# Twenty-two modulation slabs taken out of a feed-forward loop and put between attention and state-space heads

## The chip, the cores and the metric

One core of a Trainium2 chip runs the whole program. The metric is the device time of one execution in microseconds (us); the median of three executions is given. The engines are TensorE (PE, its weight loads are PEld), VectorE (DVE), ScalarE (ACT), GpSimd (POOL) and SyncE (SP), which here does nothing but issue the loads of weights.

## The reference

256 tokens of width 1024 go through two models one after the other, all in fp32. The first has two layers: a mixer (differential attention in layer 0, dilated attention with 16 heads in layer 1), cross-attention to a memory, and a feed-forward block with a gate, a convolution over three tokens and GELU. The second has two layers as well: a bidirectional state-space mixer with 32 heads in 8 groups, then a convolution module, each followed by a SwiGLU block. Each layer of the second model is steered by a *modulation*, which depends on two vectors alone (one for the context, one for the latent tokens) and not on the tokens:

```python
def ada_params(sc, w, b):
    mod = sc @ w + b            # sc (2, 1024), w (1024, 6144)
    return [t[:, None, :] for t in jnp.split(mod, 6, axis=-1)]
# sc = silu(c); one w, b for each of the two layers of the second model
h = h + g1 * mixer(rmsnorm(h, norm_mix_g) * (1 + s1) + sh1)
h = h + g2 * swiglu(rmsnorm(h, norm_ffn_g) * (1 + s2) + sh2)
```

The `w` of one layer is 24 MB. It can be multiplied at any time before that layer begins. Layer 1 of the second model begins after the state-space layer and its SwiGLU.

## The kernel before

**Slabs.** All weights lie in DRAM as 1 MB slabs of 128 partitions x 2048 floats, in the order of use. `STAGES` lists the stages and `SOURCE` the slab of each place of the stream. SP brings the stream through a ring of four buffers (`ring`). A slab is requested when PE has begun the third slab before it (`slab_begun`, counted by `begun`), so three are ahead. One slab of `ada_w` holds 256 of its 6144 columns: 24 slabs for each layer.

**Exact products.** Big projections are made of three fast passes. ACT copies a slab rounded into `w_hi` (`hi`, L2827, in two halves), POOL subtracts it from the slab into `w_lo` (`lo`, L2219, in two halves), and PE adds hi x hi, hi x lo and lo x hi (L1708, L1710, L1712): 48 matmuls of 256 columns a slab (`col_T_split`, or `col_N_split` for the other orientation; `rows_split`, L1763, for output rows). `w_lo` lies on top of the ring. In `col_T_split` the first output half takes all eight depth tiles, then the second output half does; PE waits for the first half of `w_lo` before depth tile 0 and for the second before tile 4 of the first output half. `col_N_split` waits for both halves at once.

**The modulation** isn't split. `ada` multiplies a slab as plain fp32 with a stationary operand of 32 columns (two of them hold `sc`), eight matmuls in four 32-row strips of a bank (L1939). One slab gives 2 x 256 numbers in four partial sums; DVE transposes them (`turn_ada`, L2465), ACT copies the used columns to `modC` (`ada_out`, L2880), and at the end `ada_columns` adds the strips on PE, and `modulation` adds the bias on DVE.

**Where it stands.** `f0` and `f1` are the first model's feed-forward stages, 22 slabs of its own each. Their stream alternates: one modulation slab, one feed-forward slab, 22 times; the last two of the 24 are loaded to one side (`aside`) and multiplied while a norm is computed (`late_ada`, L1950). So layer 0's modulation is in `f0`, layer 1's in `f1`. As a modulation slab has no low part, the low part of the feed-forward slab is written over its place in `w_hi` and the ring buffer is released by `lo_ready`. DVE and ACT do for each feed-forward slab: three convolution taps (L2445, L2447, L2449), GELU (L2906), product (L2454), `h_hi` (L2909), `h_lo` (L2457). `fo1` (L1763) follows. The same loop without modulation is `h0`, the SwiGLU after the state-space layer.

**Dilated heads** (loop over `q` in 0..10): for pair `q` PE makes scores (L2116) in banks 0 to 3, DVE adds the bias and takes the maximum (L2711), ACT exponentiates (L3026), DVE scales (L2727), PE transposes the weights (`weights_to_keys`, L2098, banks 4 and 5) for pair `q - 2`, ACT copies them out (L2751), and PE multiplies them with the values (L2136) for pair `q - 3` in bank 6 or 7. The output projection `rows("gwo")` (L1813) waits until banks 6 and 7 are free.

**State-space heads** (loop over head `q` in 0..31, group `g = q // 4`, place `j = q % 4`): PE makes sums (`sums`, L1442), a quarter of the gate projection (`gate_part`, L1455, plain fp32; 16 matmuls a group, into bank 3 or 7 by turns), at `j` 1 turns tokens (L1466), at `j` 2 makes scores (L1474), and at odd `j` the outputs of two heads (`two_heads`, L1493). DVE: `bounded` (L812), `head` (L824, L827), at `j` 2 `combine` (L836, L846) and `inputs_of` (L786), at `j` 3 `masked_scores` (L798). ACT: `decays` (L1134 and L1140, Exp), at `j` 3 `turned` (L1104, L1107), and at `j` 0 after `decays` the gate's Silu of the group before (`gate_of`, L1124). Silu and Exp need different tables.

## Time and profile before

| | |
|---|---|
| median of 3 executions | 2055.17 us (2053.49 to 2056.4) |
| profiled execution | 2055.43 us, its span 2053.7 us |
| busy in the span | PE 1920.8 us (94%), POOL 1252.0 (61%), DVE 1109.8 (54%), ACT 998.6 (49%) |
| moved by DMA | 342.30 MB, mean 167 GB/s |
| granted clock of TensorE | 0.977 of full speed over the span |

The profile is of one execution. PE's busy time is modelled, since matmuls overlap, so a matmul of "280 ns" may follow the one before it by less than half of that; the pitch between starts is what counts. fp32 matmuls leave two records each. Idle time of an engine counts only where the engine is the one that is waited for, which the chain of work that ended last shows.

### The profile page before, as it was taken

How to read it: one execution, taken by the hardware profiler on the slowest of the kernel's cores; microseconds unless marked ns; L12 is line 12 of the kernel's file. 1: busy time of each engine (PE TensorE's matmuls, PEld its weight loads, DVE VectorE, ACT ScalarE, POOL GpSimd, SP SyncE). 2: the span in 40 equal slices, each digit the busy share in tenths (PEclk: the TensorE clock that was granted, in tenths of full speed). 3: DMA queues.
4: the chain of work that ended last, by engine and by line, in shares of the span. 5: the costliest groups of instructions: out<-in, count | busy, mean ns of one | idle time of the engine just before them, and what ended most of it. 6: DMA issues, size and time to landing. Idle time of an engine off the chain costs nothing.

```text
span 2053.7 us, 34088 instructions
## 1 busy us (share of the span) xinstructions
PE 1920.8 (94%) x13629; PEld 1700.4 (83%) x13629; DVE 1109.8 (54%) x1524; ACT 998.6 (49%) x1726; POOL 1252.0 (61%) x585
## 2 busy tenths in 40 slices
PE   7989999999999989989999899898789999999997
PEld 7879799887999866868888788876579988968996
DVE  5472346623700172146667655678728962847981
ACT  4654345543444373435543444377845545525542
POOL 8768467686888405456778344300369886417995
PEclk9999999999999999999999899999999999999999
DMA  7435377774555405357764122211245554324552
GB/s 259 144 129 203 120 269 308 303 264 167 185 186 185 143 1 183 146 218 299 313 257 146 64 81 86 99 64 62 82 154 184 184 185 147 120 82 159 195 187 104
DMA packets 49217, 342.30 MB, mean 167 GB/s; under 512 B 5264, under 2 KB 7312, under 8 KB 8144
## 3 DMA queue, kind: packets, MB, share of 16 engines
q1 hardware_dynamic: 47440, 331.02, 44.1%
q0 software_dynamic: 1664, 9.70, 1.2%
q8 instruction: 80, 1.31, 0.3%
q14 instruction: 33, 0.27, 0.0%
HBM read 339.65 MB, written 1.05 MB: 166 GB/s over the span
## 4 chain that ended last, share of the span: by engine, by line
PE 77%; DVE 11%; ACT 6%; POOL 3%; issue 2%; DMA 1%; DVEq 0%; SPq 0%; ACTq 0%; POOLq 0%
PE bank L1708 13%; PE bank L1712 13%; PE bank L1763 13%; PE bank L1710 12%; PE bank L1813 3%; PE bank L1743 2%; PE bank L1742 2%; PE bank L1740 2%; PE bank L1939 2%; PE bank L1309 2%; PE bank L1311 2%; PE bank L1312 2%; ACT arena L1140 2%; DVE arena L723 2%; PE bank L1531 1%
## 5 line engine op out<-in xcount | busy, mean ns | idle before, releaser
L2219 POOL TENSOR_TENSOR w_lo<-ring,w_hi 128x1024 fp32r<-128x1024 f32 x360 | 877.0, 2465 | 275.2 <-ACT w_hi L2827 258.0
L1708 PE MATMUL bank<-x_hi,w_hi 128*128 128x256 f32 x2176 | 618.5, 284 | 18.6 <-POOL w_lo L2219 14.1
L1712 PE MATMUL bank<-x_lo,w_hi 128*128 128x256 f32 x2176 | 619.7, 285 | 0.0
L2827 ACT ACTIVATE w_hi<-ring 128x1024 fp32r<-128x1024 f32 x448 | 448.9, 1052 | 332.8 <-DMA ring<-slabs_dram 326.1
L1708 PEld LDWEIGHTS bank<-x_hi,w_hi 128*128 128x128 f32 x2176 | 415.8, 191 | 38.5 <-issue 37.3
L1712 PEld LDWEIGHTS bank<-x_lo,w_hi 128*128 128x128 f32 x2176 | 415.0, 191 | 0.0
L1710 PE MATMUL bank<-x_hi,w_lo 128*128 128x256 f32 x1472 | 414.3, 281 | 0.0
L1710 PEld LDWEIGHTS bank<-x_hi,w_lo 128*128 128x128 f32 x1472 | 282.4, 192 | 0.0
L2219 POOL TENSOR_TENSOR w_hi<-ring,w_hi 128x1024 fp32r<-128x1024 f32 x88 | 208.8, 2394 | 102.7 <-ACT w_hi L2827 102.7
L2751 ACT ACTIVATE arena<-bank 128x512 f32<-128x512 f32 (+1 forms) x178 | 97.9, 563 | 279.6 <-PE bank L1712 192.1
L1710 PE MATMUL bank<-x_hi,w_hi 128*128 128x256 f32 x704 | 197.5, 281 | 0.0
L416 POOL TENSOR_TENSOR w_lo<-ring,w_half 128x1024 fp32r<-128x1024 f32 x32 | 77.7, 2432 | 112.8 <-ACT w_half L1027 112.7
L1710 PEld LDWEIGHTS bank<-x_hi,w_hi 128*128 128x128 f32 x704 | 133.3, 189 | 0.0
L723 DVE SCALAR_TENSOR_TENSOR arena<-bank,pt,arena 128x508 f32<-128x508 f32 (+3 forms) x128 | 87.2, 682 | 60.1 <-ACT arena L1042 56.5
L1763 PE MATMUL bank<-w_hi,h_hi 128*128 128x512 f32 x352 | 111.9, 395 | 4.1 <-POOL w_lo L2219 1.9
L1763 PE MATMUL bank<-w_lo,h_hi 128*128 128x512 f32 x352 | 111.4, 394 | 0.0
L1763 PE MATMUL bank<-w_hi,h_lo 128*128 128x512 f32 x352 | 111.1, 393 | 0.0
L2432 DVE TENSOR_TENSOR arena<-arena 128x256 f32<-128x256 f32 x44 | 96.9, 2202 | 23.8 <-ACT arena L2899 14.5
L2457 DVE TENSOR_TENSOR h_lo<-arena,h_hi 128x256 f32 (+1 forms) x44 | 90.6, 2059 | 33.3 <-ACT h_hi L2909 33.3
L1309 PE MATMUL bank<-s_hi,w_half 128*128 128x512 f32 (+1 forms) x288 | 104.7, 363 | 1.9 <-DVE s_lo L655 1.9
L2711 DVE CUSTOM_DVE_ANT_0 arena<-bank,dist 128x512 f32<-128x512 f32 x32 | 22.1, 692 | 148.9 <-PE bank L2116 148.3
L1312 PE MATMUL bank<-s_hi,w_lo 128*128 128x512 f32 (+1 forms) x288 | 102.2, 355 | 0.0
(355 smaller groups left out, 3665.1 us busy)
## 6 DMA issues: line engine op xcount, KB each, us to landing
ring<-slabs_dram SPq DMA_DIRECT2D x308, 1024.0 KB, 4.8
lnrow<-ln_dram POOLq DMA_DIRECT2D x6, 1024.0 KB, 5.3
arena<-slabs_dram SPq DMA_DIRECT2D x4, 1024.0 KB, 8.3
xt<-xT_dram SPq DMA_DIRECT2D x1, 1024.0 KB, 5.9
xt<-memT_dram SPq DMA_DIRECT2D x1, 1024.0 KB, 12.0
x<-x_dram SPq DMA_DIRECT2D x1, 1024.0 KB, 13.6
arena<-ctx_dram POOLq DMA_DIRECT2D x1, 1024.0 KB, 8.0
lnrow<-ln_dram POOLq DMA_DIRECT2D x2, 512.0 KB, 5.0
```

Source lines behind the costliest of these rows:

```text
L723: ins = v.scalar_tensor_tensor(out=d3[:, :, lo:hi], in0=s3[:, :, lo + o:hi + o], scalar=pt[:, scw + k * 32 + j:scw + k * 32 + j + 1], in1= ...
L1309: ins = pe.matmul(dst, wh[:, k, :], hi_(k), start=(k == 0), stop=False)
L1312: ins = pe.matmul(dst, wl[:, k, :], hi_(k), start=False, stop=(k == KC - 1))
L1708: ins = pe.matmul(dst, wh[:, k, c], src[0][:, k, :], start=(k == 0), stop=False)
L1710: ins = pe.matmul(dst, wl[:, k, c], src[0][:, k, :], start=False, stop=False)
L1712: ins = pe.matmul(dst, wh[:, k, c], src[1][:, k, :], start=False, stop=(k == KC - 1))
L1763: ins = pe.matmul(bank[2 * tt + h][:, :], st, w[:, k, h * 512:(h + 1) * 512], start=(first and n == 0), stop=(end and n == 2))
L2219: pool.tensor_tensor(dst[:, c], ring[:, s, c], w_hi[:, s, c].bitcast(F32), ALU.subtract).then_inc(S["lo_ready"], 1)
L2432: step(v.tensor_tensor(act[:, u, :], act[:, u, :], val, ALU.mult))
L2457: v.tensor_tensor(h_lo[:, j, :], act[:, u, :], h_hi[:, j, :].bitcast(F32), ALU.subtract).then_inc(S["hT_ready"], 1)
L2751: a.activation(dst, bank[b][:, :] if src is None else src, ACT.Copy if not kw else ACT.Identity, **kw).then_inc(free["act"][b], 1)
L2827: a.activation(w_hi[:, g % RING, c], ring[:, g % RING, c], ACT.Copy) \
```

## The change

Layer 0's modulation stays where it is. Layer 1's 24 slabs leave `f1`:

- ten (`a1`) are multiplied in the dilated heads, one at the head of each of the iterations 0 to 9;
- two stay aside and are multiplied during the norm as before (`late_rows`);
- twelve (`sa0` to `sa7`, two and one by turns) are multiplied in the state-space heads at `j` 0. The gate projection has `j` 1 to 3 instead of 0 to 3 (5, 5 and 6 of its 16 matmuls) and bank 3 alone, and ACT's `gate_of` stands ahead of `decays` at `j` 0.

`sc_in` is laid out with zeros on both sides, so that a window of 32 columns puts the two `sc` columns at any of 16 places (`sc_at`); the sums of up to 16 slabs gather in one bank. Each group of slabs then needs one copy by ACT, two small matmuls by PE (`columns_of`) and one bias addition by DVE (`mod_rows`), in place of a transpose and a copy for each slab. In the dilated heads bank 7 holds the sums, so that L2136 has bank 6 alone.

`f1` becomes a plain stage like `h0`: 22 slabs, low parts in `w_lo`. POOL's low parts around it: slab 0's is made before the two calls of `rstd` of that norm, slab 1's after them; before, the first feed-forward slab's stood ahead of them, at the second place of the stream.

Apart from that, `col_T_split` and `col_N_split` go by depth halves: the first four depth tiles of both output halves, then the last four of both.

```diff
+def ada_slab(layer, j):
+    return AT[f"f{layer}"] + (2 * j if j < FC else 2 * FC + j - FC)
+DIL_ADA = 10
+LATE_ADA = (10, 11)
+HEAD_ADA = [2, 1, 2, 1, 2, 1, 2, 1]
...
+    if _name == "gwo":
+        STAGES.append(("a1", [ada_slab(1, j) for j in range(DIL_ADA)]))
+    if _name == "sz":
+        for _g, _k in enumerate(HEAD_ADA):
+            STAGES.append((f"sa{_g}", [ada_slab(1, _next + u) for u in range(_k)]))
+            STAGES.append((f"sz{_g}", [AT["sz"] + _g]))
+            _next += _k
+    elif _name == "f1":
+        STAGES.append((_name, [AT["f1"] + 2 * u + 1 for u in range(FC)]))
...
+        def sc_at(k, place):
+            return sc_in[:, 32 * k + 30 - 2 * place:32 * k + 62 - 2 * place]
...
+        def mod_group(v, L, b, first, n):
+            v.wait_ge(full["dve"][b], L.filled(b))
+            mod_rows(v, b, 0, first, n).then_inc(free["dve"][b], 1)
+            v.wait_ge(free["dve"][b], L.freed(b))
...
             for q in range(SH + 4):                     # ACT, state-space heads
                 g, j = q // 4, q % 4
+                if j == 0 and g >= 1:
+                    gate_of(g - 1)
                 if q < SH:
                     decays(q)
                 if j == 3 and g + 1 < SG:
                     across_scores(g + 1)
-                if j == 0 and g >= 1:
-                    gate_of(g - 1)
+                if q == SH - 2:
+                    copy_out(7, head_kept, bank[7][:, 0:T])
...
-                zb, ch = (3, 7)[g % 2], j // 2          # PE, gate_part
-                for k in range(4 * (j % 2), 4 * (j % 2) + 4):
+                for n in range((0, 5, 10)[part], (5, 10, 16)[part]):
...
                 sums(q)
-                gate_part(g, j)
+                if j == 0:
+                    modulation_part(g)
+                else:
+                    gate_part(g, j - 1)
...
             for j in range(6):                          # PE, swo
+                if j == 2:
+                    pe.wait_ge(free_of(7), frees(7))
+                    fill(columns_of(head_kept, 7, 0), 7, "dve")
...
-                for ch in range(2):                     # col_T_split
-                    col_T_half(stage, u, ch, b, src, used_up, waits, last_net)
+                for at in (0, HC):
+                    for ch in range(2):
+                        col_T_half(stage, u, ch, b, src, used_up, waits, last_net,
+                                   range(at, at + HC), True)
...
+            def ada_into(b, w, place, first, end):
+                for k in range(KC):
+                    q = 32 * (k % 4)
+                    ins = pe.matmul(bank[b][q:q + 32, 0:256], sc_at(k, place), w[:, k, :],
+                                    start=(first and k < 4), stop=(end and k >= 4))
+                    begun(ins, k == 0)
+                return ins
+            def columns_of(kept, b, at):
+                for c in range(2):
+                    ins = pe.matmul(bank[b][:, at + 32 * c:at + 32 * (c + 1)],
+                                    kept[:, c * P:(c + 1) * P], pick, start=True, stop=True)
+                return ins
...
-                    for u in range(4):                  # PE, network
-                        ada(stage, 2 * u, u, 2 * i)
-                        col_T_split(stage, 2 * u + 1, u, waits=turned if u == 0 else None)
+                if layer:
+                    with L.rounds(5, per):
+                        for u in range(4):
+                            col_T_split(stage, u, u, waits=turned if u == 0 else None)
...
             for q in range(pairs + 3):                  # PE, dilated heads
+                if q < DIL_ADA:
+                    ins = ada_into(7, slab("a1", q).rearrange("p (k c) -> p k c", k=KC), q, q == 0,
+                                   q == DIL_ADA - 1)
+                    if q == DIL_ADA - 1:
+                        fill(ins, 7, "act")
...
-                    b = 6 + k % 2
+                    k, b = q - 3, 6
...
-            rows("gwo", 4, goT)
+            rows("gwo", 4, goT, hook=dil_columns)
...
                 if k == 4:                              # POOL
-                    lo("f1", 1)
+                    lo("f1", 0)
                 rstd()
                 rstd()
+                if k == 4:
+                    lo("f1", 1)
...
-                    if conv is not None:                # DVE, network
+                    if conv == 0:
                         turn_ada(u)
...
-                    ada_out(u, j)                       # ACT, network
+                    if layer == 0:
+                        ada_out(u, j)
...
+            copy_out(7, dil_kept, bank[7][:, 0:T])      # ACT, after the dilated heads
```

## Rows read from the trace of the kernel before

**Rows 1.** The page, section 4: shares of the chain that ended last, by engine.
```profile
PE 77%; DVE 11%; ACT 6%; POOL 3%; issue 2%; DMA 1%; DVEq 0%; SPq 0%; ACTq 0%; POOLq 0%
```

**Rows 2.** Windows: stretch, length; busy us PE, PEld, DVE, ACT, POOL; clock, DMA, GB/s.
```profile
700.00:771.00 71.00, 57.07 (x558) 48.07 (x557) 46.82 (x130) 45.69 (x107) 0.00 (x0) 0.93 0.05 16
901.00:1047.00 146.00, 145.48 (x1344) 129.98 (x1344) 89.46 (x124) 73.14 (x114) 98.26 (x42) 0.99 0.78 305
1340.00:1482.00 142.00, 121.53 (x784) 91.78 (x782) 113.08 (x163) 113.58 (x283) 18.09 (x11) 1.00 0.19 68
```

**Rows 3.** The chain that ended last, in f1: start, us, what.
```profile
930.75 1.00 PE bank L1939 x16
937.60 1.00 PE bank L1939 x16
```

**Rows 4.** Timeline of one slab of f1 (start, us, engine).
```profile
946.22 0.54 DVE L2445 TENSOR_SCALAR arena<-bank,pt 128x256 f32<-128x256 f32 x1 [0.19 <-DVE arena L2465]
947.40 4.75 POOL L2219 TENSOR_TENSOR w_hi<-ring,w_hi 128x1024 fp32r<-128x1024 f32 x2 [2.14 <-ACT w_hi L2827]
949.89 2.53 DVE L2457 TENSOR_TENSOR h_lo<-arena,h_hi 128x256 f32 x1 [0.79 <-ACT h_hi L2909]
```

**Rows 5.** Timeline of h0: the same step of two slabs in a row.
```profile
1583.61 0.43 DVE L2432 TENSOR_TENSOR arena<-arena 128x256 f32<-128x256 f32 x1 [0.21 <-DVE h_lo L2434]
1589.17 0.42 DVE L2432 TENSOR_TENSOR arena<-arena 128x256 f32<-128x256 f32 x1
```

**Rows 6.** Timeline of the norm ahead of f1.
```profile
884.56 4.75 POOL L2219 TENSOR_TENSOR w_hi<-ring,w_hi 128x1024 fp32r<-128x1024 f32 x2 [6.21 <-ACT w_hi L2827]
890.09 0.75 DVE L2385 SCALAR_TENSOR_TENSOR x<-bank,small,lnrow 128x512 f32<-128x512 f32 x1 [2.22 <-POOL small L2198]
```

**Rows 7.** Timeline of PE at the start of fo1.
```profile
1057.73 0.70 PE L1763 MATMUL bank<-w_hi,h_hi 128*128 128x512 f32 x2 [0.35 <-DVE arena L2454]
```

**Rows 8.** Timeline of PE in the dilated heads.
```profile
715.62 2.03 PE L2116 MATMUL bank<-arena 64*128 64x256 f32 x24 [1.86 <-DVE small L2711]
724.62 3.58 PE L2116 MATMUL bank<-arena 64*128 64x256 f32 x24
738.66 2.03 PE L2116 MATMUL bank<-arena 64*128 64x256 f32 x24
744.91 2.03 PE L2116 MATMUL bank<-arena 64*128 64x256 f32 x24
759.20 1.06 PE L2098 MATMUL bank<-ident,arena 128*128 128x128 f32 x8 [1.74 <-ACT arena L2751]
```

**Rows 9.** Timeline of the state-space heads, one group: ACT, then PE, DVE.
```profile
1384.40 0.60 ACT L1134 ACTIVATE dist<-bank 128x512 f32<-128x512 f32 x1 [2.87 <-DVE arena L812]
1388.69 0.60 ACT L1134 ACTIVATE dist<-bank 128x512 f32<-128x512 f32 x1 [0.44 <-DVE arena L812]
1390.97 1.28 ACT L1124 ACT_TABLE_LOAD   x1
1392.88 1.28 ACT L1134 ACT_TABLE_LOAD   x1
1387.06 1.89 PE L1455 MATMUL bank<-xlat,ring 128*128 128x256 f32 x8
1388.79 0.60 PE L1466 MATMUL bank<-ident,arena 128*128 128x128 f32 x4
1390.47 1.08 PE L1493 MATMUL bank<-xt,arena 128*64 128x256 f32 x8 [1.08 <-DVE tri L827]
1392.78 0.51 PE L1442 MATMUL bank<-acT,pair_sum 128*128 128x256 f32 x2
1393.93 0.69 DVE L812 TENSOR_TENSOR arena<-bank,arena 128x512 f32<-128x512 f32 x1
```

**Rows 10.** The chain of the same group: the step that follows.
```profile
1396.55 0.97 DVE arena L827
```

**Rows 11.** Timeline of PE at the very start of the program.
```profile
23.48 0.39 PE L1708 MATMUL bank<-x_hi,w_hi 128*128 128x256 f32 x1 [0.94 <-POOL w_lo L2219]
```

More of the change, by code:

```diff
@@ L1118, in gate_of @@
             def gate_of(g):
-                zb = (3, 7)[g % 2]
-                a.wait_ge(full["act"][zb], L.filled(zb))
+                a.wait_ge(full["act"][3], L.filled(3))
                 if g >= 2:
                     a.wait_ge(S["ssq_ready"], g - 1)
-                a.activation(ring_z[g % 2], bank[zb][:, :].rearrange("p (c t) -> p c t", c=2),
-                             ACT.Silu).then_inc(free["act"][zb], 1)
-                L.freed(zb)
+                a.activation(ring_z[g % 2], bank[3][:, :].rearrange("p (c t) -> p c t", c=2),
+                             ACT.Silu).then_inc(free["act"][3], 1)
+                L.freed(3)
             def decays(q):
@@ L1938, in ada, with late_rows @@
                     q = 32 * (k % 4)
-                    ins = pe.matmul(bank[b][q:q + 32, 0:256], sc_in[:, k, :], w[:, k, :],
+                    ins = pe.matmul(bank[b][q:q + 32, 0:256], sc_at(k, 0), w[:, k, :],
                                     start=(k < 4), stop=(k >= 4))
                 fill(ins, b, "dve")
+            def ada_into(b, w, place, first, end):
[10 more added lines that the diff above has]
+                return ins
+            def late_rows(e):
+                pe.wait_ge(aside_landed[e], 32)
+                if e == 0:
+                    pe.wait_ge(free_of(7), frees(7))
+                for k in range(KC):
+                    q = 32 * (k % 4)
+                    ins = pe.matmul(bank[7][q:q + 32, 0:256], sc_at(k, e), aside[e][:, k, :],
+                                    start=(e == 0 and k < 4), stop=(e == 1 and k >= 4))
+                if e == 1:
+                    fill(ins, 7, "act")
+                    marks["late_rows"] = L.now(("act", 7))
             def late_ada(layer, e):
@@ L1971, in ada_columns @@
                                         start=True, stop=True)
+                    else:
+                        ins = pe.matmul(part[:, 0:2 * FC, :], pick, kept[:, q, 0:2 * FC, :],
+                                        start=True, stop=True)
+                if layer:
+                    pe.wait_ge(free["act"][7], marks["late_rows"])
+                    ins = columns_of(late1_kept, 4, 128)
                 fill(ins, 4, "dve")
@@ L2268, in _ @@
                 if k == 4:
-                    marks["lo_f1"] = L.now(("took", "hi_ready"))
-                    lo("f1", 1)
+                    lo("f1", 0)
                 rstd()
@@ L2790, in x_to_T @@
                             late_out(tt)
+                        if rows_at and b == 7:
+                            copy_out(7, late1_kept, bank[7][:, 0:T])
                         a.wait_ge(full["act"][b], L.filled(b))
@@ L2913, in network @@
                     L.n.update({("product", b): done[b] for b in range(4)})
-                    L.n.update({("turned", b): done[b] for b in (5, 6)})
                     per = {(k, b): 1 for k in ("net", "product") for b in range(4)} | {
-                        ("turned", 5): 2, ("turned", 6): 2, ("took", "pre_ready"): 4}
-                    hi(net, 3)
+                        ("took", "pre_ready"): 4}
+                    if layer == 0:
+                        L.n.update({("turned", b): done[b] for b in (5, 6)})
+                        per |= {("turned", 5): 2, ("turned", 6): 2}
+                        hi(net, 3)
                 else:
```

215 lines of the change are left out of this document (125 added, 90 removed).

## The prediction

> **What bounds the kernel now.** I read the page first, then a table of windows by stage, then inside the stages that the change touches the chain of waits and the timeline. The chain that ended last is 77% PE [rows 1], and the windows tell the stages apart [rows 2]. In `f1` PE is busy for 145.48 of 146 us while the next engine, POOL, has 98.26: there PE's work is the time, and what is taken out shortens it until another engine comes up. In the dilated heads (57.07 of 71 us) and the state-space heads (121.53 of 142) PE has gaps, so one might think that slabs go in for nothing. But a busy share says nothing on where the gaps lie; that takes the timelines.
>
> **f1: what goes.** In the chain a modulation slab's matmuls begin at 930.75 and 937.60: one pair of slabs takes 6.85 us, 1.00 of it the modulation's [rows 3]. What is the pitch without it? `h0` is the same loop with the same 48 matmuls a slab; its product on DVE comes at 1583.61 and 1589.17, pitch 5.56 [rows 5]. That is 1.29 less, more than the 1.00: the change between the two kinds of matmul costs too. I take 5.56: 22 x (6.85 - 5.56) = **28.4 us less**.
>
> Will another engine hold `f1` above 5.56? POOL needs 4.75 a slab [rows 4]. The stream needs one load of 1 MB in 5.56 us where it now has two in 6.85 at 305 GB/s [rows 2]. DVE is the one to look at: from the first tap of a slab at 946.22 to the end of `h_lo` at 949.89 + 2.53 = 952.42 it takes 6.20 us in one string [rows 4], with waits for ACT inside, and DVE takes the slabs strictly in turn. Laid end to end, these strings would hold `f1` at 6.20. But look at `h_lo` itself: 2.53 us for 256 columns, where the first tap of as many columns takes 0.54. It starts 2.49 us after POOL's pair of subtractions and ends 0.27 after them (947.40 + 4.75 = 952.15): it stands waiting for POOL's second subtraction to end [rows 4]. So its end hangs on POOL's beat, not on its own start; it can start up to about 2 us later for nothing. With POOL at one pair a slab, DVE lags by 0.8 us and stays there. (The Trainium skill, "SBUF — State Buffer", Who interferes with whom, says the same in general: a VectorE instruction with two SBUF inputs and a GpSimd one that reads SBUF exclude each other, and the second to be issued waits for the whole of the first. By that rule alone one could also fear that each `h_lo` costs DVE a full subtraction, which makes the first rival below; the row's end, just behind POOL's, agrees with the rule and not with that fear.)
>
> **Around f1.** In the norm ahead, POOL does its two subtractions from 884.56 to 889.31 and only then the `rstd` that DVE waits 2.22 us for [rows 6]. The new order asks for slab 0's low part before it, and as the stream has no modulation slab ahead, that slab is requested one slab of output rows earlier and POOL is done with it in time: **-2.2**. At the end of `f1` PE now waits 0.35 us for DVE's last product [rows 7]; with DVE 0.8 behind and PE's last slab not followed by anything to cover that, I take **+0.9**. The late slabs, the columns and the addition of the bias stay beside the norm and the output rows. Sum for `f1`: -29.7.
>
> **Dilated heads: what comes.** Scores start at 738.66 and 744.91, 6.25 us a pair [rows 8]. The cycle is: scores, DVE's maximum, ACT's exponential and copy, PE's transposes, scores again. Each waits for the one before, and the slab is put between transposes and scores, on that cycle: 1.00 an iteration at the price of [rows 3]; the ends are 0 (a gap covers it) and 1.29. It is covered where PE waits anyway right there or just before: 1.86 us at `q` 2, about as much at `q` 1, and 1.74 ahead of the transposes of `q` 8 [rows 8]. Seven of ten remain: +7.0. Then `rows` waits for bank 7 too, whose copy is ACT's last: half the width of the 0.60 us read in [rows 9], so +0.4; two matmuls of 32 columns, +0.2 (four of 128 take 0.60, [rows 9]). Against this stands the clock: it is 0.93 over this stage [rows 2], and scores that take 2.03 us took 3.58 in one of the stretches at half clock [rows 8]. All of it is worth (1 - 0.93) x 71 x 0.8, 4 us. Slabs in the gaps before `q` 1 and 2 may remove some: -1.0. Together **+6.6**; DMA moves 16 GB/s here [rows 2], so that a slab every 7 us is there in time.
>
> **State-space heads.** The slab itself comes after PE's sums at `j` 0, in the place of 1.9 us of gate work; what counts is the single bank 3. PE may begin the gate's next part only after ACT's Silu of the group before. ACT, counted from the start of `decays` at `j` 3 (1384.40): it has finished `turned` at 1388.69 - 0.44, after 3.85 us; the gate's table and Silu take 1392.88 - 1390.97 = 1.91; bank 3 is free at 5.76. Until then PE has the end of two heads (by which it runs some 1.8 behind that start once a group has this order), twice the sums (0.51 each) and one or two slabs (1.00 each): 4.8 at most. **The slabs cost nothing** here. From 5.76 PE does five matmuls (ten records at (1388.79 - 1387.06) / 8: 2.16), the tokens (0.5), two heads (1392.78 - 1390.47 = 2.31) and the sums of `j` 2 (0.51), with starts in between 0.1: 11.34. DVE bounds them and multiplies, 0.69 and 0.03 twice: its L827 starts at 12.78 [rows 9]. Before, it started at 1396.55, after 12.15 [rows 10]. So a group grows by 0.63, seven times: +4.4; behind L827 all is as before. ACT's own path gets shorter by the 0.44 that it waited. With one copy on ACT and two small matmuls again (+0.6): **+5.0**. Ends: 7 x -0.44 = -3.1, if PE keeps up, and 12.0 for the slabs on top.
>
> **Depth halves.** At the start PE waits 0.94 us for POOL's fourth half, with 12 of 48 matmuls of that slab done [rows 11]; with 24 to do before that wait, it is gone: **-0.9**. Elsewhere PE doesn't wait for a second half, and the order costs nothing: the matmuls are the same.
>
> **Sum.** Loop -28.4, norm -2.2, end +0.9, so -29.7; with +6.6, +5.0 and -0.9 that is -19.0 on the profiled execution's 2055.43 (its span is 2053.7, the rest lies around it), thus 2036.4; the median of the runs, 2055.17, is 0.3 below that execution. I say **2036.3 us**.
>
> **Rivals.**
> 1. *DVE's string sets f1* (6.20 a slab, above): the loop saves 14.3 instead of 28.4: 2050.4. For it: 6.20 is measured; against: the end of `h_lo` hangs on POOL. Chance 0.14.
> 2. *The gaps take everything:* PE keeps up in the state-space heads (-3.1 instead of +4.4) and the dilated heads get the whole clock back (3 more): 2025.8. For it, PE's gaps in [rows 2]; against, the walk above. 0.09.
> 3. *The slabs cost their full price in the state-space heads too,* because their PE time delays sums that DVE needs: +12, 2048.3. PE has 121.53 of 142 us filled already. 0.11.
> 4. *Slower:* the gate on ACT now stands ahead of `decays`. Should bank 3 be filled only after ACT arrives, ACT stands at the head of its queue, and DVE and PE, which need the decays, behind it. Then gate, table (1.28), slabs (1.5 a group) and 0.63 add up: 5.3 x 7 = 37 instead of 4.4: 2069. It decides against the change from 3.9 us a group on ((19.0 + 4.1) / 7 + 0.63). Against it: the last gate part ends more than 4 us before ACT gets there. 0.04.
>
> Rivals 1 and 3 together (2062) have 0.02; my forecast 0.60, by itself 2030 to 2042.
>
> **Range and chances.** From rival 2 to rival 1: 2026 to 2051. Under 0.2% (4.1 us) is no change that a measurement of this kernel can tell. Faster: forecast, rivals 2 and 3 and most of 1, 0.89; within: the rest of 1 and mixtures of 1 with parts of 3, 0.05; slower: 0.06.
>
> **What would show it.** In the profile after: starts of a `f1` slab 5.56 us apart (6.2 would be rival 1) with `h_lo` ending just behind POOL's pair; scores of the dilated heads 7.2 us apart; PE waiting for ACT before the first gate part of a group and L827 0.6 later per group, no wait of ACT for bank 3; `rstd` ahead of `f1` without DVE's 2.2 us; no wait for POOL in the second slab of the program. I would be wrong by most if DVE and POOL fall into another beat in `f1`.

## The result: slower, and the profile after

The changed kernel takes 2067.05 us (median; 2066.77 to 2069.39), the kernel before on the same chip 2054.49: ratio 1.0063, 95% interval 1.0045 to 1.0080. That is 12.6 us slower where I had forecast 19 less. The profiled execution has a span of 2064.7 us, against 2053.7.

The stages show where it went. Each number is the start of the first matmul of a stage on PE's timeline, in us. The third column is the run of the first experiment, told below, and the fourth the best kernel of the study.

| stage begins | before | after | arena back | best |
|---|---|---|---|---|
| last values ahead of the dilated heads (`gv`) | 682.25 | 689.47 | 681.55 | 681.82 |
| `xv1`, behind the dilated heads | 798.16 | 810.07 | 803.53 | 803.90 |
| `f1` | 903.39 | 911.02 | 902.57 | 902.95 |
| `fo1` | 1054.37 | 1040.70 | 1026.64 | 1027.06 |
| `h0`, behind the state-space heads | 1534.39 | 1532.03 | 1518.99 | 1507.35 |
| `ho0` | 1660.17 | 1662.30 | 1643.67 | 1632.86 |
| `h1` | 1855.79 | 1860.20 | 1840.86 | 1830.46 |
| `ho1` | 1981.28 | 1991.73 | 1966.62 | 1954.92 |
| span | 2053.7 | 2064.7 | 2039.1 | 2027.4 |

`f1` did become shorter, by 21.3 us (150.98 to 129.68). But time is lost in places where no work was added: 7.2 us ahead of the dilated heads, 4.5 in `h0`, 6.0 in `h1`. To see why, look at one stretch in which PE never waits, eight slabs of `gq` and `gk`: 384 matmuls, then the first of the next projection. PE's timeline of before:

```profile
570.47 0.28 PE L1708 MATMUL bank<-x_hi,w_hi 128*128 128x256 f32 x1
614.84 0.28 PE L1740 MATMUL bank<-w_hi,x_hi 128*128 128x256 f32 x1
```

and of after:

```profile
573.92 0.28 PE L1768 MATMUL bank<-x_hi,w_hi 128*128 128x256 f32 x1
620.40 0.28 PE L1806 MATMUL bank<-w_hi,x_hi 128*128 128x256 f32 x1
```

44.37 / 384 is 115.5 ns from one matmul to the next; 46.48 / 384 is 121.0. Same instructions, same count, the full granted clock in both. Each one's own duration (0.28) does not show it; only the distance between starts does. The changed kernel multiplies 114 slabs of this kind: 114 x 48 x 5.5 ns is 30 us. The 16 slabs of the other orientation (`col_N_split`) went the other way: the four behind this stretch take 23.04 us before (614.84 to 637.88) and 22.61 after (620.40 to 643.01), 120.0 and 117.8 ns a matmul. The wide matmuls changed too, whose code is untouched: the chain of `ho0` of before, of after, and of a later run (the arena 64 bytes lower), one row each.

```profile
1660.17 59.91 PE bank L1763 x258
```

```profile
1662.30 60.44 PE bank L1831 x258
```

```profile
1656.39 58.76 PE bank L1831 x258
```

That untouched code changed its pace was the hint that the order of the matmuls is not it.

The rest of the profile after, against the forecast. The chain that ended last, by engine, with 75% on PE where it had 77% [rows 1]:

```profile
PE 75%; DVE 10%; POOL 5%; issue 4%; ACT 4%; DMA 1%; DVEq 0%; POOLq 0%; SPq 0%; ACTq 0%
```

In `f1`, POOL's pair of subtractions and DVE's `h_lo` of one slab [rows 4]: `h_lo` stretches to 965.24 and ends 0.28 us behind the pair (960.19 + 4.77). DVE still hangs on POOL's beat, as forecast. The loop takes 129.68 / 22 = 5.89 us a slab, where I had 5.56.

```profile
960.19 4.77 POOL L2339 TENSOR_TENSOR w_lo<-ring,w_hi 128x1024 fp32r<-128x1024 f32 x2 [1.03 <-ACT w_hi L2949]
963.21 2.03 DVE L2577 TENSOR_TENSOR h_lo<-arena,h_hi 128x256 f32 x1 [0.80 <-ACT h_hi L3032]
```

In the norm ahead of `f1` [rows 6], POOL is done early and DVE's first product with `rstd` follows without a wait for it:

```profile
891.45 4.76 POOL L2339 TENSOR_TENSOR w_lo<-ring,w_hi 128x1024 fp32r<-128x1024 f32 x2 [0.60 <-ACT w_hi L2949]
900.51 0.75 DVE L2505 SCALAR_TENSOR_TENSOR x<-bank,small,lnrow 128x512 f32<-128x512 f32 x1
```

In the dilated heads [rows 8] scores are 7.25 us apart, where they were 6.25:

```profile
740.05 2.02 PE L2229 MATMUL bank<-arena 64*128 64x256 f32 x24
747.30 2.02 PE L2229 MATMUL bank<-arena 64*128 64x256 f32 x24
754.54 2.03 PE L2229 MATMUL bank<-arena 64*128 64x256 f32 x24
```

In the state-space heads [rows 9, 10] the chain goes from ACT's Silu (L1165, first its table) to PE's gate (L1499). A group with two slabs, then one with a single slab:

```profile
1392.34 1.28 ACT L1165
1393.63 0.61 ACT xt L1165
1394.38 2.40 PE bank L1499 x10
1396.77 0.44 PE bank L1519 x4
1397.21 2.31 PE bank L1546 x24
...
1447.93 1.28 ACT L1165
1449.22 0.61 ACT xt L1165
1449.96 4.03 PE bank L1499 x10
1453.99 2.31 PE bank L1546 x24
```

PE's timeline has its wait for the Silu in the same two groups:

```profile
1394.38 2.40 PE L1499 MATMUL bank<-xlat,ring 128*128 128x256 f32 x10 [1.51 <-ACT xt L1165]
1449.96 4.03 PE L1499 MATMUL bank<-xlat,ring 128*128 128x256 f32 x10 [2.37 <-ACT xt L1165]
```

The same ten records (five matmuls) take 2.40 us and 4.03: there PE comes back at half its clock (1.2 GHz). This happens in two of the six groups that wait, both with one slab and a wait of some 2.4 us; the third such group (at 1376.40) kept the full clock, and so did all three with two slabs and a wait of 1.51. And at the output projection behind these heads, whose first slab began at the full clock in the kernel before, PE stands for 5.08 us and then is slow again. PE's timeline, and the chain from there:

```profile
1469.11 1.19 PE L1587 MATMUL bank<-w_swo,yT_hi 128*128 128x512 f32 x2 [5.08 <-ACT xt L1165]
```

```profile
1469.11 7.95 PE bank L1587 x24
1477.06 2.31 PE bank L1546 x24
1479.37 5.79 PE bank L1587 x24
```

### The profile page after: what moved, and what is told of

It reads as the page before. It is cut to its first block, busy times and chain, and to the rows that moved or that the text cites. A ratio compares the mean times of both kernels' runs of the same rounds, so it can differ in the third digit from the quotient of the medians.

```text
span 2064.7 us, 33951 instructions
## 1 busy us (share of the span) xinstructions
PE 1945.6 (94%) x13633; PEld 1728.1 (84%) x13633; DVE 1007.8 (49%) x1502; ACT 996.1 (48%) x1703; POOL 1249.3 (61%) x585
## 4 chain that ended last, share of the span: by engine, by line
PE 75%; DVE 10%; POOL 5%; issue 4%; ACT 4%; DMA 1%; DVEq 0%; POOLq 0%; SPq 0%; ACTq 0%
PE bank L1831 13%; PE bank L1768 12%; PE bank L1771 11%; PE bank L1774 11%; POOL w_lo L2339 4%; PE bank L1881 3%; PE bank L1809 2%; PE bank L1811 2%; PE bank L1806 2%; PE bank L1353 2%; PE bank L1355 2%; PE bank L1356 2%; PE bank L1587 2%; DVE arena L765 2%; PE bank L1499 1%
## 5 line engine op out<-in xcount | busy, mean ns | idle before, releaser
L2339 POOL TENSOR_TENSOR w_lo<-ring,w_hi 128x1024 fp32r<-128x1024 f32 x404 | 979.4, 2452 | 329.3 <-ACT w_hi L2949 311.7
L1768 PE MATMUL bank<-x_hi,w_hi 128*128 128x256 f32 x2176 | 628.4, 289 | 17.2 <-POOL w_lo L2339 13.0
L1771 PE MATMUL bank<-x_hi,w_lo 128*128 128x256 f32 x1824 | 520.8, 286 | 0.0
L1768 PEld LDWEIGHTS bank<-x_hi,w_hi 128*128 128x128 f32 x2176 | 419.5, 193 | 27.8 <-issue 27.7
L1771 PEld LDWEIGHTS bank<-x_hi,w_lo 128*128 128x128 f32 x1824 | 351.9, 193 | 0.0
L2339 POOL TENSOR_TENSOR w_hi<-ring,w_hi 128x1024 fp32r<-128x1024 f32 x44 | 104.5, 2397 | 48.5 <-ACT w_hi L2949 48.5
L1355 PE MATMUL bank<-s_lo,w_half 128*128 128x512 f32 (+1 forms) x288 | 102.0, 354 | 0.0
L1771 PE MATMUL bank<-x_hi,w_hi 128*128 128x256 f32 x352 | 98.8, 281 | 0.0
L497 POOL TENSOR_TENSOR dist<-dist,xt 128x512 f32<-128x512 f32 x8 | 10.6, 1325 | 144.4 <-ACT xt L1146 144.4
L2577 DVE TENSOR_TENSOR h_lo<-arena,h_hi 128x256 f32 (+1 forms) x44 | 78.2, 1777 | 33.6 <-ACT h_hi L3032 33.6
```

The costliest lines, as they stand in the source:

```text
L1355: pe.matmul(dst, wh[:, k, :], lo_(k), start=False, stop=False)
L1768: ins = pe.matmul(dst, wh[:, k, c], src[0][:, k, :], start=(k == 0 and (ch == 0 or not both)), stop=False, skip_group_check=both)
L1771: ins = pe.matmul(dst, wl[:, k, c], src[0][:, k, :], start=False, stop=False, skip_group_check=both)
L2339: pool.tensor_tensor(dst[:, c], ring[:, s, c], w_hi[:, s, c].bitcast(F32), ALU.subtract).then_inc(S["lo_ready"], 1)
L2577: v.tensor_tensor(h_lo[:, j, :], act[:, u, :], h_hi[:, j, :].bitcast(F32), ALU.subtract).then_inc(S["hT_ready"], 1)
```

## Experiments on the place of the arrays

`w_hi` and `x_hi` (the rounded weights and activations), `h_hi` and `h_lo` lie in the arena; the remainders `w_lo` and `x_lo` lie in the slab ring and in the triangle tile, which are allocated before `small` and did not move. The conditioning tile `sc_in` grew from 256 to 286 floats and `small` shrank from 576 to 552. After rounding up to 32 bytes the arena begins at byte 114,656 instead of 114,624. Four kernels tell this place from the order of the matmuls.

**Arena back** (e1; changed kernel, constants packed):

```diff
-small = sb("small", [P, 552])
+small = sb("small", [P, 544])
-pick = small[:, 264:296]
+pick = small[:, 248:280]
-lamp = small[:, 296:424]
+lamp = small[:, 280:408]
-dtn = small[:, 296:552]
+dtn = small[:, 280:536]
```

> The changed kernel, with the small constants packed 8 floats tighter, so that the turned latent and the arena (w_hi, x_hi, h_hi and most else) lie at the byte they had before the change; the changed kernel has them 32 bytes further (114,656 in place of 114,624 bytes), because the conditioning tile grew from 256 to 286 floats and the small tile shrank by 24 only. No instruction differs. Theory place (the 32 bytes make the split projections' matmuls start every 121.0 instead of 115.6 ns): the triples of L1768 go back to 0.347 us, 114 slabs x 48 x 5.4 ns = 29.5 us less, so about 2038 us. Theory order (multiplying by halves of the depth makes them slow): same as the changed kernel, 2067 us within 2.

Measured: 2040.99 us, ratio 0.9946 (0.9930 to 0.9963). It computes with the same instructions as the changed kernel at other addresses, and it is faster than the kernel before.

**The new order in the kernel before** (e3; its `col_T_half`, `col_T_split`, `col_N_split` replaced by the changed kernel's):

```diff
-for ch in range(2):
-    col_T_half(...)
+for at in (0, HC):
+    for ch in range(2):
+        col_T_half(..., range(at, at + HC), True)
```

> The kernel before with the depth-half order of the split projections alone (both output halves of one bank in turn for depth chunks 0 to 3, then for 4 to 7), nothing else. Theory order: its 92 projection slabs outside the two feed-forwards go from 115.6 to 121.0 ns a matmul, 92 x 48 x 5.4 ns = 24 us more, about 2078 us. Theory place: the pitch stays at 115.6 ns, and the start comes out 0.9 us sooner, 2053.5 us within 1.5.

Measured: 2053.67 us, ratio 0.9998 (0.9989 to 1.0008), the same stretch at 115.6 ns (44.38 / 384). The order slows nothing.

**The kernel before, arena 32 bytes on** (e2):

```diff
-small = sb("small", [P, 576])
+small = sb("small", [P, 584])
```

> The kernel before with the small tile 8 floats longer and no other edit, so that the turned latent and the arena start 32 bytes further, where the changed kernel has them. Theory place: 92 slabs x 48 x 5.4 ns = 24 us more, less 18 slabs x 48 x 2.1 ns = 1.8 us in the projections with tokens as columns, plus some 2 ns in each of about 1,000 wide matmuls, so about 2078 us. Theory order: no difference, 2054.5 us within 2.

Measured: 2075.01 us, ratio 1.0103 (1.0087 to 1.0120), 121.0 ns. Eight unused floats cost this kernel some 21 us.

**The old order in the changed kernel** (e4; the second edit reversed; every address as changed):

> The changed kernel with its split projections in the order of the kernel before (all eight depth chunks of one output half, then of the other), everything else and every address as changed. Theory order: the pitch goes back from 121.0 to 115.6 ns, 114 x 48 x 5.4 ns = 29.5 us less, plus the 0.9 us of the start, about 2039 us. Theory place: 121 ns stays, 2068 us within 2. If both had a part, this run and the one with the arena back would share the 29 us between them.

Measured: 2072.22 us, ratio 1.0091 (1.0074 to 1.0108), 121.0 ns. Theory order falls. The old order is even 5 us worse by the medians, more than the 0.9 of the start, though the two intervals touch (1.0074 to 1.0108 against 1.0045 to 1.0080). The same with the arena back (e5):

> The changed kernel with the arena back at its old byte and the split projections in the order of the kernel before (one output half, then the other). Compared with the changed kernel whose arena is back (2041.0 us), it is the order of the matmuls alone. In the changed kernel with the arena 32 bytes on, the old order cost 5.2 us (2072.2 against 2067.0), in the kernel before the new order gave nothing (2053.67 against 2053.65). Theory wait (the new order lets a projection begin on half a slab where the remainders of the weights are only just done, which is so now that the first-layer loop runs at 5.6 us a slab): about 2045 to 2046 us. Theory none (what the arena's place added is gone, and with it what the order gave): 2041 us within 1.5.

Measured: 2047.30 us, ratio 0.9961 (0.9948 to 0.9973), against 0.9946 (0.9930 to 0.9963): 3 us by the ratios, 6 by the medians, with intervals that overlap, so that its size is not settled. Its `f1` begins 2.2 us later than with the new order and ends 6.5 later (1033.16); in that loop PE waits for GpSimd's subtraction of `w_lo` five times, 2.2 us in all, which the new order's loop does not do. In the kernel before, a slab of modulation stood between two projections; I read it as what gave POOL that time, but no run separates this.

Then: which array, and what about 32 bytes?

**`w_hi` alone** (e8; on the arena-back kernel):

```diff
-arena = sb("arena", [P, 28672])
+arena = sb("arena", [P, 28680])
-w_hi = part("w_hi", arena_at + 4 * 20480, RING, SLAB)
+w_hi = part("w_hi", arena_at + 4 * 20488, RING, SLAB)
```

> The changed kernel with the arena back (2041.0 us), and of its arrays w_hi alone (the rounded weights) 32 bytes further, the arena 8 floats longer for it; x_hi, m_hi, h_hi and all else stay. Theory stationary (the projections with tokens as rows of the result load their weights from w_hi, and this load is what the 32 bytes slow): the pitch of L1768 to L1774 goes from 115.6 to 121 ns, 114 x 48 x 5.4 ns, so about 2067 us. Theory moving (it is the moving operand, x_hi of 1 KB a partition): the pitch stays at 115.6 ns, about 2041 us, and only the wide matmuls of L1831, where w_hi is the moving operand, take 2 ns more, 1 to 2 us in all.

Measured: 2051.38 us, ratio 0.9985 (0.9975 to 0.9994), 117.8 ns. Neither theory: 10 of the 26 us by the medians, 8 of 24 by the ratios.

**All of the arena 64 bytes lower** (e10; constants packed by 16 floats more), and, with `w_hi` put back on the byte it had in the arena-back kernel, **`x_hi` alone** 32 bytes off its own (e9; the rest of the arena stays 64 bytes lower):

```diff
-small = sb("small", [P, 544])
+small = sb("small", [P, 528])
```

```diff
-x_hi = part("x_hi", arena_at + 4 * 18432, KC, T)
+x_hi = part("x_hi", arena_at + 4 * 18440, KC, T)
-w_hi = part("w_hi", arena_at + 4 * 20480, RING, SLAB)
+w_hi = part("w_hi", arena_at + 4 * 20496, RING, SLAB)
```

> The changed kernel with its small constants packed tighter still, so that the turned latent and the arena start 64 bytes below the place that gave 2041.0 us, and 96 below the changed kernel's. Theory boundary (what counts is whether the arrays begin on a multiple of 64 bytes): pitch 115.6 ns and 2041 us within 2. Theory distance (it is the distance to the arrays that did not move, the weights' and the activations' remainders, in the slab ring and the triangle tile): another pitch, 118 to 121 ns, 2050 us or more.

> The changed kernel with the arena on a 64-byte boundary (2041.0 us with it 32 bytes back), and x_hi alone, the rounded activations that are the moving operand of the projections, 32 bytes off that boundary; w_hi lies 64 bytes further than in that kernel, all the rest 64 bytes lower. With w_hi alone 32 bytes off the boundary the pitch went from 115.6 to 117.8 ns and the time to 2051.4. Theory sum (each operand that lies 32 bytes off costs its own part): the pitch goes to 118 to 119 ns, 114 x 48 x 2.4 to 3.4 ns = 13 to 19 us, so 2054 to 2060 us. Theory pair (it is w_hi and x_hi standing 32 bytes off the two remainders, or off each other, that counts): anything from 2041 to 2051 us; equal to the 2051.4 us of w_hi alone if only their distance matters.

Measured: 2057.23 us, ratio 1.0012 (1.0002 to 1.0021), and 2055.86 (2053.44 to 2064.32), 1.0011 (0.9999 to 1.0022), both at 120.0 ns. In e9 the pitch is above what either theory gave, though the time lies in the range of theory sum. `x_hi` alone, 32 bytes lower, costs 4.5 ns, where `w_hi` alone, 32 higher, cost 2.3 and both 32 higher 5.5; no run has `x_hi` alone 32 higher, so it stays open whether such parts add up. The first, e10, ends the notion of a 64-byte boundary: moved by 64 bytes, the projections are slow again, while the wide matmuls become faster than in any kernel so far (58.76 us for 258, the third row above). Its stretch on PE's timeline:

```profile
573.54 0.28 PE L1768 MATMUL bank<-x_hi,w_hi 128*128 128x256 f32 x1
619.62 0.28 PE L1806 MATMUL bank<-w_hi,x_hi 128*128 128x256 f32 x1
```

Is it the place of an array, or its distance from the ones that stayed? Two kernels on the fastest version (told in the next section) move the others; 64 bytes taken out of the constants leave the arena at byte 114,624:

```diff
+sb("pad", [P, 16])
 ring_at = aligned()        # e13: ring, triangle tile and all between
```

```diff
+sb("pad", [P, 16])
 tri_at = aligned()         # e14: triangle tile (x_lo) and what follows it
```

> The kernel of 2029.7 us (arena back, gate late, last heads first) with 64 bytes put ahead of the slab ring and 64 taken out of the small constants, so that ring (w_lo), triangle tile (x_lo) and all between lie 64 bytes further and the arena (w_hi, x_hi, h_hi, h_lo) where it was, at byte 114,624. The distance between the rounded arrays and the remainders is now as in the kernel whose arena lay 64 bytes lower (2057.2 us, every triple's matmuls 120.0 ns apart), while w_hi and x_hi lie at the byte that gave 115.6 ns. Theory distance: 120.0 ns a matmul in the projections and 227 ns in the wide ones, 16 us more than 2029.7, about 2046 us. Theory place (the byte of w_hi and x_hi themselves): 115.6 ns and 2030 us within 2.

> As the run before it, but the 64 bytes stand ahead of the triangle tile, behind the slab ring: x_lo lies 64 bytes further, w_lo, w_hi and x_hi lie where the kernel of 2029.7 us has them. Theory distance of the moving pair (x_hi against x_lo): the pitch is 120.0 ns or near it, about 2046 us. Theory distance of the weights' pair (w_hi against w_lo), or place: 115.6 ns stays, 2030 us within 2. Part of each would give a time between. The wide matmuls of the feed-forwards read neither of the two and stay at 231 ns in every case.

Measured: 2047.63 us, ratio 0.9958 (0.9941 to 0.9975), 120.0 ns; and 2041.68, 0.9929 (0.9912 to 0.9945), 117.8 ns, against 0.9880 for the base. So it is largely the distance: with `w_hi` and `x_hi` at the byte that was good, but `w_lo` and `x_lo` 64 bytes further, 18 us by the medians are lost (16 by the ratios), and the pace is that of e10, whose arrays have the same distances at other bytes. The other orientation and the wide matmuls agree with e10 as well (table). The wide ones of e13 in the chain:

```profile
1648.94 58.76 PE bank L1831 x258
```

It is not the weights' pair alone that decides, since moving `x_lo` alone costs 12 of the 18 us (10 of 16), though it touches only one of the pairs; theory distance of that pair alone, with 120.0 ns, is not borne out either. What e13 shows in PE's timeline:

```profile
575.29 0.28 PE L1768 MATMUL bank<-x_hi,w_hi 128*128 128x256 f32 x1
621.37 0.28 PE L1806 MATMUL bank<-w_hi,x_hi 128*128 128x256 f32 x1
```

All in one table; "pitch" is the length of the stretch from its first matmul to the first of the next projection, divided by 384, from the same two rows in each run's timeline. "Other" is the same for the 192 matmuls of the other orientation behind it, and "wide" the time of the 258 wide matmuls of `ho0` in the chain. The offsets are the start bytes modulo 128, a unit that I chose because 114,624 and 16,512 differ by 64 in it; the runs do not prove that it is the period.

| run | w_hi | x_hi | w_lo | x_lo | pitch, ns | other, ns | wide, us |
|---|---|---|---|---|---|---|---|
| before, arena back, e3, best | 64 | 64 | 0 | 0 | 115.5 to 115.6 | 120.0 | 59.87 to 59.91 |
| e8 | 96 | 64 | 0 | 0 | 117.8 | 117.2 | 59.60 |
| e14 | 64 | 64 | 0 | 64 | 117.8 | 117.8 | 59.89 |
| e9 | 64 | 32 | 0 | 0 | 120.0 | 117.8 | 60.02 |
| e10 | 0 | 0 | 0 | 0 | 120.0 | 120.0 | 58.76 |
| e13 | 64 | 64 | 64 | 64 | 120.0 | 120.0 | 58.76 |
| after, e2, e4 | 96 | 96 | 0 | 0 | 121.0 | 117.8 | 60.43 to 60.44 |

## Experiments on the state-space heads

With the arena back, the stretch from `fo1` to `h0` still takes 492.35 us where it took 480.02: +12.3, for which I had +5.0.

**One bank for the gate, alone, in the kernel before** (e6). No slabs:

```diff
-zb, ch = (3, 7)[g % 2], j // 2         # four matmuls in each of the four steps
+for n in range((0, 5, 10)[part], (5, 10, 16)[part]):   # bank 3, steps 1 to 3
 ...
-                if q < SH:
-                    decays(q)
                 if j == 0 and g >= 1:
                     gate_of(g - 1)
+                if q < SH:
+                    decays(q)
```

> The kernel before with one part of the change alone: in the state-space heads the gate's projection has bank 3 for every group and no longer banks 3 and 7 in turn, sixteen matmuls in steps 1 to 3 of a group (5, 5, 6) and none in step 0, and ScalarE's Silu stands ahead of the decays of a group's first head and not behind them. No slab is multiplied there, all else as before. Theory bank (the single bank, on which TensorE waits until the Silu of the group before has read it, is what costs the changed kernel 12 us in these heads): the group's period goes from 17.06 to about 17.9 us, 7 x 0.9 = 6 us, with up to two groups longer by 1.6 at half clock, so 2060 to 2063 us. Theory slabs (the slabs' 1.0 us in a group's step 0 is what costs): 2054 to 2055 us. My forecast had 4.4 us for the gate's part, 2058 us.

Measured: 2074.08 us, ratio 1.0096 (1.0079 to 1.0113): 19.7 us slower than before, more than with the slabs (+12.3 in this stretch), and more than theory bank gave. The chain and PE's timeline of one group:

```profile
1411.49 0.61 ACT xt L1122
1412.23 4.60 PE bank L1453 x10
1416.84 0.85 PE bank L1464 x4
1417.69 2.32 PE bank L1491 x24
...
1432.83 4.61 PE bank L1453 x10
```

```profile
1412.23 4.60 PE L1453 MATMUL bank<-xlat,ring 128*128 128x256 f32 x10 [3.08 <-ACT xt L1122]
```

PE waits 3.08 us for the Silu (1.51 with two slabs, 2.37 with one), and from here on every group's ten records behind it run at half clock; the groups are 20.60 us long. Of the three groups before, the one that waited only 0.93 us ran at full clock. The windows of the heads give the granted clock (the column behind the engines' busy times), of this kernel, of after, and of the next one:

```profile
1344.00:1493.00 149.00, 123.44 (x718) 94.11 (x718) 108.30 (x156) 107.33 (x274) 13.96 (x9) 0.88 0.15 53
```

```profile
1343.00:1470.00 127.00, 110.27 (x795) 82.68 (x794) 97.82 (x141) 96.32 (x244) 14.18 (x10) 0.96 0.36 136
```

```profile
1330.00:1449.00 119.00, 108.51 (x802) 81.04 (x800) 100.89 (x143) 95.50 (x246) 14.49 (x9) 1.00 0.41 150
```

The modulation slabs, put where PE would else have waited, kept the clock up in four of six groups. The slabs are not what costs: they hide part of what the new gate costs. This edit has three parts, though (one bank, no gate work in step 0, the Silu ahead of the decays); the next two runs leave the bank and the Silu where they are and move the gate's matmuls.

**The gate in a group's last two steps** (e7, arena back):

```diff
-for n in range((0, 5, 10)[part], (5, 10, 16)[part]):
+for n in range(8 * part, 8 * part + 8):
 ...
-if j == 0:
-    modulation_part(g)
-else:
-    gate_part(g, j - 1)
+if j < 2:
+    modulation_part(g, j)              # one slab a step
+else:
+    gate_part(g, j - 2)
```

> The changed kernel with the arena back (2041.0 us), and in the state-space heads a group's slabs in steps 0 and 1 (one in each) and its gate in steps 2 and 3, eight matmuls each, in place of slabs in 0 and gate in 1, 2, 3. TensorE then reaches bank 3 some 4 us after the Silu has read it and does not wait there. Theory bank (the wait for the Silu at the gate's first matmul is on the path): the heads give back 0.9 us in each of 7 groups and the two stretches at half clock, 6 to 9 us in all, 2032 to 2035 us. Theory work (TensorE's work of a group is the bound whatever its order, or the Silu is late by the gate's last part instead): 2039 to 2043 us.

Measured: 2035.25 us, ratio 0.9908 (0.9891 to 0.9924). Most groups are 16.81 us long (17.06 before), at a clock of 1.00. The single bank and the Silu's place are as they were; a second slab now stands in step 1. The same on the kernel before, without slabs (e12):

> The kernel before with the gate of the state-space heads in one bank (no slabs there), its sixteen matmuls in a group's last two steps, eight each; with them in steps 1 to 3 this kernel took 2074.1 us and TensorE's granted clock was 0.88 there. Theory wait (what costs is that TensorE stands waiting for the Silu and comes back at half clock; where the gate comes late enough, a single bank costs nothing but at the end): groups of about 17 us at a clock of 1.00, and some 5 us at the output projection, which still waits for bank 3: 2058 to 2061 us. Theory work (without the slabs, steps 0 and 1 leave TensorE so little to do that the clock falls anyway): groups of 18 to 20 us and 2065 us or more.

Measured: 2064.46 us (2061.59 to 2065.85), ratio 1.0049 (1.0033 to 1.0066). 10 us better than e6, from which it differs in the place of the gate's matmuls alone: half of what e6 cost was the wait at the bank and the slow clock behind it, and neither the one bank by itself nor the Silu's place. But it is 3.5 to 6.5 above what theory wait gave. Its groups are as long as theory wait had them (17.82 and 16.38 us by turns, 17.1 in the mean), and PE waits 5.0 us at the output projection; but the clock is 0.96 over its heads, where theory wait had 1.00: in every second group two heads' matmuls (24 records) take 4.07 us instead of 2.31. Theory work had the fall of the clock right, and the length of the groups not. In the profiled executions the same order takes 486.04 us from `fo1` to `h0` with slabs (e7) and 488.61 without.

**The last heads first** (e11). In the kernel with the late gate PE still stands at the output projection:

```profile
1449.03 1.19 PE L1587 MATMUL bank<-w_swo,yT_hi 128*128 128x512 f32 x2 [5.05 <-ACT xt L1165]
```

```diff
+two_heads(SH // 2 - 1)
 for b_ in (0, 1, 2, 3):
     pe.wait_ge(free_of(b_), frees(b_))
 ...
-if j == 1:
-    two_heads(SH // 2 - 1)
```

> The kernel with the arena back and the gate in a group's last two steps (2035.3 us), and one edit: the last two heads' matmuls stand ahead of the output projection of the state-space layer, where they stood behind its first slab. There TensorE sat idle for 5.05 us, because this projection begins by waiting for banks 0 to 3, and bank 3 is free only when ScalarE's last Silu has read it (in the kernel before, the last gate was in bank 7); then it ran its first 24 matmuls in 8.54 us in place of 5.74, at a granted clock of 0.73, and the last heads, on which the last four weight roundings wait, came 8 us after the Silu. Theory bank (this wait is the part of the one-bank gate that the other order left): the last heads run in the idle time, GpSimd's roundings have no gap of 5.3 us, and 4 to 5.5 us are given back, so 2030 to 2031 us. Theory end (the projection ends with four roundings that wait for slabs from memory, whatever came before): 2034 to 2036 us.

Measured: 2029.70 us, ratio 0.9880 (0.9863 to 0.9896): 25 us faster than the kernel before, 37 faster than the changed one. PE's timeline at the same place, with the last heads in the gap:

```profile
1446.40 1.08 PE L1546 MATMUL bank<-xt,arena 128*64 128x256 f32 x8 [2.66 <-DVE tri L869]
...
1448.80 0.70 PE L1588 MATMUL bank<-w_swo,yT_hi 128*128 128x512 f32 x2
```

From `fo1` to `h0` it is now 480.29 us: with twelve modulation slabs in them, this stretch takes as long as it did without. The kernel before does not have this place of the last heads, and no run gives it one; what it would save there is open.

## Why the prediction was wrong

- **The step that failed** is one sentence: "Elsewhere PE doesn't wait for a second half, and the order costs nothing: the matmuls are the same." That the order costs nothing holds (e3). But "the matmuls are the same" priced 5472 matmuls at nothing because their instructions don't change, and the sum has no term for the diff's two allocation lines. They moved the operands by 32 bytes, and this costs 26 us by the medians (2067.05 against 2040.99), 24 by the ratios. The sum by the rows is 30. In the three loops `f1`, `h0` and `h1` it comes out: 17.0 us of 17.4. The other 48 slabs should give 12.7, and the rest of the program differs by 8.6; 1.7 of the gap are the 16 slabs of the other orientation, which became faster, and what remains was not traced. The pitch of 5.56 that I carried from `h0` into `f1` fell with it: 48 matmuls at 121.0 ns are already 5.81. It was also read from one pair of slabs: the whole of `h0` takes 125.78 / 22 = 5.72 us a slab before.
- **The loop of `f1`**, -28.4 and +0.9 at its end: right in size. With the arena back it goes from 150.98 us to 124.07 (5.64 a slab), -26.9; 1.9 more (the first modulation slab ahead of it) lies before its start. Rival 1 did not happen: `h_lo` ends just behind POOL's pair, as forecast. Two reasons were off. I put what a pair of slabs saves beyond the slab's 1.00 us down to the change between two kinds of matmul. But before, the low part lay in `w_hi`'s place, and there, from the second to the last of a slab's 48 matmuls (938.75 to 944.17), they are 117.8 ns apart, against 115.5 with the low part in `w_lo`: some 0.1 of the 0.29 is again a matter of place. And what PE waits for at the loop's end is not DVE's last product but POOL:

```profile
1026.64 0.70 PE L1831 MATMUL bank<-w_hi,h_hi 128*128 128x512 f32 x2 [0.84 <-POOL w_lo L2339]
```

- **Norm**, -2.2: from the start of `xwo1`'s rows to `f1` 4.9 us went (866.81 to 903.39, and 870.87 to 902.57), 1.9 of them that slab's, so -3.0: right.
- **Dilated heads**, +6.6: from `gv`'s last slabs to `xv1` +6.1 (115.91 to 121.98), with scores 1.00 us further apart, as forecast.
- **State-space heads**, +5.0: measured +12.3. That the slabs cost nothing was right, and rival 3 is refuted: under either order of the gate the stretch is shorter with slabs than without (492.35 us against 499.89 of e6, 486.04 against 488.61 of e12), and with all twelve slabs in, e11 comes out at +0.3. Two terms were mis-sized. The walk took the ten matmul records behind the Silu at full speed (2.16) and gave a group 0.63 more; at full clock a group is 17.97 us long, 0.91 more than 17.06, and the one whose matmuls begin at half clock at 1412.35 is 19.63. e7, which takes that wait away, gave back 6.3 where I had 4.4. And "one copy on ACT and two small matmuls again (+0.6)" overlooked that the output projection begins by waiting for banks 0 to 3, one of which was now the last gate's: 5.08 us of waiting and a slow start, 5.8 by e11. I had named what waits inside a group, and not what waits behind the last one.
- **Start of the program**, -0.9: right; in e3, where nothing else differs, the first projection with tokens as columns begins 1.3 us sooner. That half slabs would help nowhere else looks wrong by a few us in the new kernel, within what e5's overlapping intervals allow: without the modulation slabs and in the old order PE waits for POOL in `f1`.
- **The sum.** Without the arena's shift the forecast of 2036.3 stands against 2040.99. That is in the range, 4.7 above, with the state-space heads 7.3 too low and the loop and the norm some 2 too high; only this is not the kernel that was to be timed. The chance of "slower", 0.06, held rival 4, which did not occur, rivals 1 and 3 together, and nothing for the memory map.

What stays open: why the distance of the arrays acts on matmuls back to back. Placements were varied in steps of 32 and 64 bytes only, the four operands not in all combinations, and no kernel has both the 115.5 ns of the projections and the 227.8 of the wide matmuls (58.76 / 258). Why the clock fell in every second group of e12 was not followed up.

## What to carry to other kernels

A change in the size of any tile shifts all that is allocated behind it: before comparing two kernels, print the addresses of the matmuls' operands, and keep them in place with padding, or try a few paddings as a tuning step of its own. When untouched code changes its pace in the trace, measure start to start over hundreds of instructions; single durations do not show it. When two uses are merged into one bank, look for every later wait for this bank, the last one behind the loop too, and prefer an order in which PE comes to the bank late: a wait of 2.4 or 3.1 us cost a second time in most groups here, when PE came back at half clock, and one of 1.51 in none.

## What the runs showed of the hardware

- The distance from matmul to matmul (128 rows, 256 columns, in groups of three) depends on the bytes at which their operands lie: 115.5, 117.8, 120.0 or 121.0 ns at the same granted clock. For 512 columns it is 232.2, 234.3 and 227.8 (59.91, 60.44 and 58.76 us for 258 in a row); what is best for the one is not for the other, nor for the other orientation (120.0 where the first has 115.5, 117.8 where it has 121.0). The Trainium skill ("TensorE: Matmul & The Clock Gate", Back-to-back issue gap) gives the gap of an isolated matmul as the columns divided by 2.4 GHz and some 2.5 ns, by which 256 columns would take an estimated 109. It adds that the spacing in a real stream is set by weight loads too, and gives about 131 ns for 512 columns. None of these rows reaches either figure, and neither section says a word on where the operands lie. The Trainium skill's page "SBUF — State Buffer", Operand start alignment, asks for no more than a start at a multiple of the element's size and says that the runs behind it timed nothing; every place tried here keeps to that, and they are up to 5% apart.
- e10 and e13 have all four arrays 64 bytes apart in place and the same distances between them, and the same pace in all three kinds of matmul (120.0 ns, 120.0 ns, 58.76 us): the difference counts.
- PE that had waited 3.08 us came back at half clock in each of the last four groups (4.60 us for ten records that take 2.40), and the mean clock was 0.88; with the wait cut to 1.51 or 2.37 us by slabs it was 0.96, and half clock came behind two of the three waits of 2.37 and none of 1.51; with the gate later as well the clock was 1.00.
